# Sums, splits and means around the output projection of a hybrid encoder layer: three reorderings

## Chip, cores and metric

The kernel runs on one core of one Trainium2 chip. The metric is the time of one execution on the device in microseconds; three runs of the kernel before gave a median of 774.31 us (773.64 to 775.06). Lower is better.

## What is computed

One layer for 512 prompt frames and 32 sample frames (544 columns; D_MODEL 1024, D_FF 4096), all in float32:

```
xn = RMSNorm(x);  [u | q | k | v | gate_a | gate_b] = xn @ w_in
A = pooling mixer(u): trailing means of 2/4/8/16 rows less the row, a 128x128 map per group, scaled
B = stick-breaking attention(q, k, v), 8 heads of 64, strictly causal, cached keys for the samples
x += (sigmoid(gate_a) * (A @ w_pool_up) + sigmoid(gate_b) * (B @ w_sb_up)) @ w_out
x += relu(RMSNorm(x) @ w_up)^2 @ w_down
x += sigmoid(RMSNorm(x) @ w_ple_gate) * (p @ w_ple_proj);  y = final RMSNorm(x)
```

## The kernel before

Features lie on the 128 partitions, the 544 columns on the free axis, in two halves of 272. Each float32 operand is split into a high part in fp32r and a low part (the rest), and TensorE does three matmuls per product: high by high, high by low, low by high. Weights come in tiles of 128x1024 (512 KB). SyncE loads a tile into a raw buffer; ScalarE copies its high part (`split` and `hi`, lines 836 to 854); VectorE subtracts it to get the low part (lines 1808 to 1822); TensorE uses it. `ahead(t)` on ScalarE and VectorE makes the parts of tile t+3; there are four tiles of parts (W_RING) and, until the MLP, two raw buffers; from there on six.

The order of work is written out by hand for each engine in one block (SyncE from line 637, GpSimd 707, ScalarE 833, TensorE 1323, VectorE 1799); the engines meet at counting semaphores alone. `full` counts results that TensorE has finished, `taken` those that VectorE has taken out of PSUM, `copied` those that ScalarE has; a result uses one of four PSUM slots, and `place_for` (line 1610) or `take` (line 1330) makes TensorE wait until the slot's former result is out.

The stages in order of time: the input projection with attention, a pair of heads at a time (`pair`: ScalarE 960, TensorE 1467, VectorE 1989); the pool projection (`pool_part`, line 1448) and the attention projection; the output projection, eight tiles w_out, q = 0 to 7; the MLP; the embedding gate; the last norm. The MLP and the gate use a scheme of seven products per 2x2 block (Strassen-Winograd), in groups of seven (`group_of`, line 1661); it needs four sums of weight quarters for each group.

**The last pair of heads.** On VectorE it ends with gate(3, i), stick(1, i), group_lo(2), group_lo(3), stick_later(1, i), a split and stick_lo(1, i) (lines 2063 to 2072). `group_lo(g)` takes the mixer map of group g out of PSUM, after ScalarE's `group_hi(g)` (line 955). `stick` takes the logarithms of the last head; then GpSimd masks them (line 763), ScalarE makes their high part (`stick_hi`), and TensorE sums them (`sums(1, PAIRS - 1)`) after the first two tiles of the pool projection.

**The sums of quarters.** GpSimd makes them in DRAM in 19 slots: `sum_copies(k)` (line 775) issues four copies of group k, once all DMAs of slot k-1 have landed; `sum_additions(k)` (line 784) issues the four additions of the groups k-1, k-2 and k-3. Slots 0 to 7 are issued in the pairs of heads, 8 to 18 in a loop over `paces` (lines 811 to 821), a pair of counts of `full` for each slot: one that its copies wait for, one that its additions wait for. Slot 9 waits for the attention projection, slot 10 for the output projection, 11 and on for every half chunk of the MLP. SyncE loads sums from there into raw buffers (`staged`, line 673), up to nine products before they are used.

**The output projection.** For each tile q, VectorE adds the result to x (`add_residual`, line 2137, "the residual" below). Then eight operands of the MLP are made from two feature tiles each: ScalarE scales x by the norm's weight (lines 1068 and 1074), VectorE forms differences (lines 2156 to 2169), ScalarE makes high parts (1071 to 1081) and a square (869), VectorE the low parts (`low`, line 2147) and the sum of squares. ORDER pairs tiles, so that even q have the operands B11 and NT1, odd q the others. The split of the weight tile q+4 stands ahead of this work on both engines: line 1089 on ScalarE (ahead of its wait for the residual), line 2153 on VectorE (behind the residual). The same helper `operand_lo` serves the last down projection with nth = 1.

In the first up group ScalarE copies the first three results out of PSUM (`copy_quarter`, line 1093), the first of these once all low operands are made (line 1151); the third product of a group adds onto the PSUM slot of the first.

Of the kernel before, what the change touches and what calls it, by code (L numbers as in the profile page):

```python
# [28 lines left out]
KT = D_MODEL // P  # L29
# [268 lines left out]
def hybrid_step_kernel(nc, w_tiles, x_t, p_t, ck_t, cv, state_t, w_grp, vecs,  # L298
# [5 lines left out]
    with ctx:  # L304
# [402 lines left out]
        def _(pool):  # L707
# [100 lines left out]
                                   base=0, pattern=[[0, HEADS], [1, DEC]], channel_multiplier=-1).then_inc(done, 1)  # L808


            paces = [(0, 0), (N_ATT, N_ATT + KT // 2), (N_OUT, N_OUT + KT // 2)]
            for c in range(CHUNKS):
                second = [NTH[("dn", c, s, 0)] for s in (0, 4)] if c < SEVENS else [NTH[("down", c, q)] for q in (0, 4)]
                paces += [(NTH[("up", 2 * c, 0)], NTH[("up", 2 * c + 1, 0)]), tuple(second)]
            for k, (copies, additions) in enumerate(paces, HEADS):
                if copies:
                    pool.wait_ge(full, copies)
# [15 lines left out]
        def _(act):  # L833
# [251 lines left out]
            act.wait_ge(blo_done, KT)  # L1085
            ahead(T_OUT)
            for q in range(KT):
                if q < KT - 1:
                    ahead(T_OUT + q + 1)
                act.wait_ge(taken, N_OUT + q + 1)  # L1090
                operand_hi(0, q, g_mlp)

            def copy_quarter(g, n, s):

# [704 lines left out]
        def _(dve):  # L1799
# [8 lines left out]
            def split(t, i=0, per=0):  # L1808

                s = t % W_RING  # L1810
                dve.wait_ge(whi_done, t + 1 + i * per)
                dve.tensor_tensor(w_lo[:, s, :, :].rearrange("p k c -> p (k c)"), raw[:, t % RAW_RING, :],  # L1812
                                  w_hi[:, s, :, :].rearrange("p k c -> p (k c)"), ALU.subtract).then_inc(wlo_done, 1)
# [80 lines left out]
            def stick(hh, i):  # L1894

                g = 2 * i + hh
                dve.wait_ge(ln_done, g + 1)
                dve.scalar_tensor_tensor(out=work[:, :], in0=z_ps, scalar=0.0, in1=work[:, :],
                                         op0=ALU.max, op1=ALU.add).then_inc(sp_done, 1)
# [89 lines left out]
            def pair(i):  # L1989
                first = isinstance(i, int) and i == 0  # L1990
                last = isinstance(i, int) and i == PAIRS - 1
                q, k, v = (ev[:, n, 0:TOK] for n in range(3))
                if not first:
                    split(AHEAD + 0, i, S1_PER)

                dve.wait_ge(full, 1 + i * S1_PER)
                dve.scalar_tensor_tensor(out=halves(q), in0=pair_result(0, i), scalar=DH ** -0.5, in1=halves(rn[:, :]),
                                         op0=ALU.mult, op1=ALU.mult).then_inc(taken, 1)
                if first:
                    normed(1, k, i, S1_PER, pair_result(1, i)).then_inc(taken, 1)  # L2000
                    normed(2, v, i, S1_PER, pair_result(2, i)).then_inc(taken, 1)
                    dve.wait_ge(taken, 3)
                if first:
                    q_parts(i)
                    k_parts(i)
                    pool_input(i)
                    split(AHEAD + 1)
                    running_q(i)
                    dve.tensor_copy(kst[:, i, :], k[:, SEQ:TOK])
                    dve.tensor_copy(vst[:, i, :], v[:, SEQ:TOK])  # L2010
                    split(AHEAD + 2)
                else:
                    running_q(i)
                    q_parts(i)
                    split(AHEAD + 1, i, S1_PER)
                    dve.wait_ge(kv_out[0], 16 * i)
                    normed(1, k, i, S1_PER, pair_result(1, i)).then_inc(taken, 1)
                    dve.wait_ge(taken, 2 + i * S1_PER)
                    dve.tensor_copy(kst[:, i, :], k[:, SEQ:TOK])
                    k_parts(i)  # L2020
                    split(AHEAD + 2, i, S1_PER)
                    prob_lo(1, i - 1)
                    dve.wait_ge(kv_out[1], 16 * i)
                    normed(2, v, i, S1_PER, pair_result(2, i)).then_inc(taken, 1)
                    dve.wait_ge(taken, 3 + i * S1_PER)
                    dve.tensor_copy(vst[:, i, :], v[:, SEQ:TOK])
                if not first:
                    head_out(1, i - 1)
                    stick(0, i)
                    split(AHEAD + 3, i, S1_PER)  # L2030
                    stick_later(0, i)

                if not first:
                    pool_input(i)
                if first:
                    stick(0, i)
                    split(AHEAD + 3)
                    stick_later(0, i)
                stick_lo(0, i)
                dve.wait_ge(vhi_done, i + 1)  # L2040
                dve.tensor_tensor(v_parts[:, :, V_LO, :], o_heads, v_parts[:, :, V_HI, :], ALU.subtract)\
                   .then_inc(vlo_done, 1)
                split(AHEAD + 4, i, S1_PER)
                gate(0, i)
                split(AHEAD + 5, i, S1_PER)
                if last:

                    dve.wait_ge(mean_done, GROUPS)
                gate(1, i)
                split(AHEAD + 6, i, S1_PER)  # L2050
                if last:
                    mean_lo(0)
                    mean_lo(1)
                prob_lo(0, i)
                gate(2, i)
                if last:
                    group_lo(0)
                head_out(0, i)
                if last:
                    group_lo(1)  # L2060
                    mean_lo(2)
                    mean_lo(3)
                    gate(3, i)
                else:
                    split(AHEAD + 7, i, S1_PER)
                stick(1, i)
                if last:
                    group_lo(2)
                    group_lo(3)
                    stick_later(1, i)  # L2070
                    split(AHEAD + 7, i, S1_PER)
                    stick_lo(1, i)
                    for s in kv_out:
                        dve.wait_ge(s, 16 * PAIRS)
                else:
                    gate(3, i)
                    stick_later(1, i)
                    stick_lo(1, i)
# [62 lines left out]
            def operand_lo(nth, q, t):  # L2141


                m, j = ORDER[q], ORDER[q] % 4
                of = 3 * (KT // 2 * nth + j)

                def low(first, last, at, made):
                    dve.wait_ge(uhi_done, made)
                    dve.tensor_tensor(u_lo[:, first:last + 1, j, :], parts[:, at:at + last - first + 1, :],
                                      u_hi[:, first:last + 1, j, :], ALU.subtract).then_inc(ulo_done, 1)  # L2150

                if q < KT - 1:
                    ahead(t + 1)
                dve.wait_ge(xg_done, KT * nth + q + 1)
                if m < 4:
                    dve.tensor_tensor(parts[:, P_NT1, :], parts[:, P_B11, :], parts[:, P_B12, :], ALU.subtract)\
                       .then_inc(t_done, 1)
                    if q:
                        add_square(q - 1, (nth + 1) * KT)
                    low(NT1, B11, P_NT1, of + 1)  # L2160
                else:
                    dve.scalar_tensor_tensor(out=parts[:, P_NT2, :], in0=parts[:, P_B22, :], scalar=-1.0,
                                             in1=parts[:, P_NT1, :], op0=ALU.mult, op1=ALU.subtract)\
                       .then_inc(t_done, 1)
                    link(dve.tensor_tensor(parts[:, P_T3, :], parts[:, P_B22, :], parts[:, P_B12, :], ALU.subtract))
                    dve.wait_ge(t_done, of + 2)
                    dve.scalar_tensor_tensor(out=parts[:, P_T4, :], in0=parts[:, P_NT2, :], scalar=-1.0,
                                             in1=parts[:, P_B21, :], op0=ALU.mult, op1=ALU.subtract)\
                       .then_inc(t_done, 1)
                    if q < KT - 1:  # L2170
                        add_square(q - 1, (nth + 1) * KT)
                    low(B21, NT2, P_B21, of + 2)
                    low(T3, T4, P_T3, of + 3)
                if q == KT - 1:
                    add_square(q - 1, (nth + 1) * KT)
                    add_square(q, (nth + 1) * KT)

            ahead(T_OUT)
            for q in range(KT):
                add_residual(N_OUT + q, ORDER[q])  # L2180
                operand_lo(0, q, T_OUT + q)

            def add_quarter(g, n, s):

# [369 lines left out]
```

## Time and profile before

| | |
|---|---|
| median of three runs | 774.31 us (773.64 to 775.06) |
| the profiled execution: its own time | 772.34 us |
| its span, first to last instruction | 770.6 us |
| TensorE busy | 754.8 us, 5902 matmuls |
| VectorE busy | 556.9 us |
| ScalarE busy | 422.0 us |
| GpSimd busy | 147.2 us |
| mean granted TensorE clock | 0.996 |

PE is TensorE, DVE VectorE, ACT ScalarE, POOL GpSimd. Times in a timeline are from the start of the span. A name like L2139 is a line of the kernel; `x2` merges neighbouring instructions. In brackets stands how long the engine was idle before the instruction and what released it.

### The profile page before, as it was taken

The numbers are of one execution on the slowest core, as the hardware profiler recorded it, in microseconds if no ns is written. First come the engines' busy times: TensorE is split into PE (matmuls) and PEld (weight loads), VectorE is DVE, ScalarE is ACT, GpSimd is POOL, SyncE is SP. The second block draws the span as 40 slices with busy tenths as digits, with TensorE's granted clock in tenths as the row PEclk, the third lists the DMA queues.
The fourth block names the chain that finished last, engine by engine and source line by source line (L and its number), as shares of the span: only waits on it lengthen the run. The fifth ranks groups of instructions, "written<-read, shape, count | busy, mean of one in ns | idle before, by whom it ended". The sixth has DMA issues, their size and how long they took to land.

```text
span 770.6 us, 14459 instructions
## 1 busy us (share of the span) xinstructions
PE 754.8 (98%) x5902; PEld 746.2 (97%) x5902; DVE 556.9 (72%) x705; ACT 422.0 (55%) x524; POOL 147.2 (19%) x259
## 2 busy tenths in 40 slices
PE   9999999999999999999999999999999999999994
PEld 9999999999999999999999999999999999999993
DVE  6776556566567527588998669965998667677986
ACT  7545535435485442477674347634763356556575
POOL 1051342453471332021110111111101000000001
PEclk9999999999999999999999999999999999999998
DMA  7254848769779899988797989789776957342503
GB/s 242 93 181 140 233 147 224 225 193 262 218 179 265 259 242 275 292 267 262 213 299 270 236 329 251 282 232 354 207 243 201 278 185 217 105 117 66 204 1 116
DMA packets 49516, 165.78 MB, mean 215 GB/s; under 512 B 6320, under 2 KB 8368, under 8 KB 49456
## 3 DMA queue, kind: packets, MB, share of 16 engines
q1 hardware_dynamic: 28512, 94.16, 35.6%
q0 software_dynamic: 18688, 67.18, 35.5%
q10 hardware_dynamic: 2256, 3.60, 1.4%
q8 instruction: 43, 0.70, 0.4%
q14 instruction: 17, 0.14, 0.1%
HBM read 160.39 MB, written 71.63 MB: 301 GB/s over the span
## 4 chain that ended last, share of the span: by engine, by line
PE 90%; DVE 5%; ACT 3%; issue 1%; DMA 1%; SPq 0%; POOL 0%; POOLq 0%; DVEq 0%
PE psum L1646 23%; PE psum L1697 16%; PE psum L1345 14%; PE psum L1351 14%; PE psum L1348 14%; PE psum L1394 1%; PE psum L1422 1%; DMA xt<-x_t 1%; PE psum L1420 1%; PE psum L1382 1%; PE psum L1381 1%; ACT xt L1265 1%; PE psum L1401 1%; PE psum L1406 1%; ACT L879 0%
## 5 line engine op out<-in xcount | busy, mean ns | idle before, releaser
L853 ACT ACTIVATE w_hi<-raw_more 128x1024 fp32r<-128x1024 f32 x83 | 87.7, 1056 | 72.3 <-PE psum L1697 43.3
L1345 PE MATMUL psum<-a_hi,w_hi 128*128 128x272 f32 x576 | 120.6, 291 | 0.6 <-DVE w_lo L1812 0.5
L1820 DVE TENSOR_TENSOR w_lo<-raw_more,w_hi 128x1024 fp32r<-128x1024 f32 x83 | 101.1, 1222 | 26.1 <-ACT w_hi L853 25.7
L1351 PE MATMUL psum<-a_hi,w_lo 128*128 128x272 f32 x576 | 119.3, 289 | 0.0
L1348 PE MATMUL psum<-a_lo,w_hi 128*128 128x272 f32 x576 | 118.9, 288 | 0.0
L1646 PE MATMUL psum<-u_hi,w_hi 128*128 128x272 f32 x560 | 116.4, 289 | 1.0 <-ACT h_of L1097 1.0
L1646 PE MATMUL psum<-u_hi,w_lo 128*128 128x272 f32 x560 | 115.8, 289 | 0.0
L1646 PE MATMUL psum<-u_lo,w_hi 128*128 128x272 f32 x560 | 115.7, 288 | 0.0
L1345 PEld LDWEIGHTS psum<-a_hi,w_hi 128*128 128x128 f32 x576 | 90.3, 189 | 1.1 <-DVE w_lo L1812 0.7
L1348 PEld LDWEIGHTS psum<-a_lo,w_hi 128*128 128x128 f32 x576 | 90.5, 189 | 0.0
L1351 PEld LDWEIGHTS psum<-a_hi,w_lo 128*128 128x128 f32 x576 | 90.0, 189 | 0.0
L1646 PEld LDWEIGHTS psum<-u_hi,w_hi 128*128 128x128 f32 x560 | 87.9, 188 | 1.7 <-issue 1.2
L1646 PEld LDWEIGHTS psum<-u_lo,w_hi 128*128 128x128 f32 x560 | 88.3, 189 | 0.0
L1646 PEld LDWEIGHTS psum<-u_hi,w_lo 128*128 128x128 f32 x560 | 87.4, 188 | 0.0
L1812 DVE TENSOR_TENSOR w_lo<-raw,w_hi 128x1024 fp32r<-128x1024 f32 x41 | 51.2, 1250 | 43.3 <-ACT w_hi L845 43.1
L1820 DVE TENSOR_TENSOR w_lo<-raw,w_hi 128x1024 fp32r<-128x1024 f32 x44 | 53.6, 1222 | 19.2 <-ACT w_hi L853 12.3
L789 POOL DMA_DIRECT2D sums_t<-sums_t x32 | 27.5, 1013 | 207.1 <-PE psum L1646 87.9
L1348 PE MATMUL psum<-b_lo,w_hi 128*128 128x272 f32 x304 | 62.9, 288 | 0.0
L853 ACT ACTIVATE w_hi<-raw 128x1024 fp32r<-128x1024 f32 x39 | 41.2, 1056 | 36.0 <-PE psum L1697 21.6
L1345 PE MATMUL psum<-b_hi,w_hi 128*128 128x272 f32 x288 | 60.0, 290 | 0.0
L782 POOL DMA_DIRECT2D sums_t<-w_tiles x64 | 33.6, 535 | 135.5 <-DMA sums_t<-w_tiles 97.7
L1351 PE MATMUL psum<-b_hi,w_lo 128*128 128x272 f32 x288 | 59.4, 287 | 0.0
(287 smaller groups left out, 1553.0 us busy)
## 6 DMA issues: line engine op xcount, KB each, us to landing
sums_t<-w_tiles POOLq DMA_DIRECT2D x96, 512.0 KB, 8.2
raw<-w_tiles SPq DMA_DIRECT2D x63, 512.0 KB, 4.4
raw_more<-sums_t SPq DMA_DIRECT2D x42, 512.0 KB, 5.8
raw_more<-w_tiles SPq DMA_DIRECT2D x41, 512.0 KB, 4.5
sums_t<-sums_t POOLq DMA_DIRECT2D x32, 512.0 KB, 11.1
raw<-sums_t SPq DMA_DIRECT2D x22, 512.0 KB, 6.0
xt<-x_t SPq DMA_DIRECT2D x8, 272.0 KB, 5.7
y_t<-xt SPq DMA_DIRECT2D x16, 136.0 KB, 1.9
```

What stands on the lines that cost most here:

```text
L782: pool.dma_start(sum_tile(i, what), sum_tile(i, of)).then_inc(sums_in, 16)
L789: pool.dma_start(sum_tile(i, what), sum_tile(i, of), accum_op=ALU.add).then_inc(sums_in, 16)
L853: act.activation(w_hi[:, t % W_RING, :, :].rearrange("p k c -> p (k c)"), src, ACT.Copy)\
L1265: act.activation(x, x, ACT.Copy, scale=g_fin[:, m:m + 1]).then_inc(xg_last, 1)
L1345: pe.matmul(base[:, h, :], w_hi[:, s, wk, :], at(hi, k, h * HALF, (h + 1) * HALF), start=(opens and q == 0), stop=False, skip_group_check= ...
L1348: pe.matmul(base[:, h, :], w_hi[:, s, wk, :], at(lo, k, h * HALF, (h + 1) * HALF), start=False, stop=False, skip_group_check=True)
L1351: mm = pe.matmul(base[:, h, :], w_lo[:, s, wk, :], at(hi, k, h * HALF, (h + 1) * HALF), start=False, stop=(closes and q == len(ks) - 1), s ...
L1381: pe.matmul(z, b_lo[:, keys], b_hi[:, both], start=(b != 3), stop=False, skip_group_check=True)
L1646: mm = pe.matmul(out[:, two, :], w_part[:, t % W_RING, 2 * k + two, :], u_part[:, op, k, :], start=(OPENS[s] and k == 0 and w_part is w_hi ...
L1697: mm = pe.matmul(out[:, two, :], w_part[:, t % W_RING, 2 * k + two, :], h_part[:, i * HALF:(i + 1) * HALF], start=(OPENS[s] and k == 0 and ...
L1812: dve.tensor_tensor(w_lo[:, s, :, :].rearrange("p k c -> p (k c)"), raw[:, t % RAW_RING, :], w_hi[:, s, :, :].rearrange("p k c -> p (k c)" ...
L1820: dve.tensor_tensor(w_lo[:, t % W_RING, :, :].rearrange("p k c -> p (k c)"), src, w_hi[:, t % W_RING, :, :].rearrange("p k c -> p (k c)"), ...
```

## The change

The constants of the slots' waits are written anew: counted in products from the start of the MLP, with `at(c, j)` the j-th product of chunk c, and no slot waits for the output projection any more. On ScalarE and VectorE the split of tile q+4 in the output projection moves behind the operand work of tile q. In the last pair of heads group_lo(2) moves ahead of stick(1).

```diff
@@ -808,10 +808,18 @@
-            paces = [(0, 0), (N_ATT, N_ATT + KT // 2), (N_OUT, N_OUT + KT // 2)]
-            for c in range(CHUNKS):
-                second = [NTH[("dn", c, s, 0)] for s in (0, 4)] if c < SEVENS else [NTH[("down", c, q)] for q in (0, 4)]
-                paces += [(NTH[("up", 2 * c, 0)], NTH[("up", 2 * c + 1, 0)]), tuple(second)]
+            def at(c, j):
+
+                if j < 2 * T_UP:
+                    return NTH[("up", 2 * c + j // T_UP, j % T_UP)]
+                j -= 2 * T_UP
+                return NTH[("dn", c, j // 2, j % 2)]
+
+            paces = [(0, 0), (N_ATT, N_ATT + KT // 2)]
+            paces += [(at(0, 0), at(0, 6)), (at(0, 12), at(0, 18)), (at(0, 24), at(1, 1)), (at(1, 6), at(1, 12)),
+                      (at(1, 18), at(1, 23)), (at(2, 2), at(2, 8)), (at(2, 14), at(2, 20)),
+                      (at(3, 2), at(3, 8)), (NTH[("down", 3, 0)], NTH[("down", 3, 4)])]
             for k, (copies, additions) in enumerate(paces, HEADS):
                 if copies:
                     pool.wait_ge(full, copies)
@@ -1085,10 +1093,11 @@
             for q in range(KT):
+                act.wait_ge(taken, N_OUT + q + 1)
+                operand_hi(0, q, g_mlp)
+
                 if q < KT - 1:
                     ahead(T_OUT + q + 1)
-                act.wait_ge(taken, N_OUT + q + 1)
-                operand_hi(0, q, g_mlp)
@@ -2063,9 +2072,11 @@
+                if last:
+
+                    group_lo(2)
                 stick(1, i)
                 if last:
-                    group_lo(2)
                     group_lo(3)
                     stick_later(1, i)
                     split(AHEAD + 7, i, S1_PER)
@@ -2149,7 +2160,7 @@
-                if q < KT - 1:
+                if nth and q < KT - 1:
                     ahead(t + 1)
                 dve.wait_ge(xg_done, KT * nth + q + 1)
@@ -2179,6 +2190,8 @@
             for q in range(KT):
                 add_residual(N_OUT + q, ORDER[q])
                 operand_lo(0, q, T_OUT + q)
+                if q < KT - 1:
+                    ahead(T_OUT + q + 1)
```

## Rows read from the trace of the kernel before

**Rows 1.** The page: busy time of TensorE; its granted clock in 40 slices.

```profile
PE 754.8 (98%) x5902; PEld 746.2 (97%) x5902; DVE 556.9 (72%) x705; ACT 422.0 (55%) x524; POOL 147.2 (19%) x259
...
PEclk9999999999999999999999999999999999999998
```

**Rows 2.** Waits of TensorE: us in total, times, longest.

```profile
PE psum L1781 <- ACT h_two L1310: 1.9, 1, 1.9
...
PE psum L1646 <- ACT h_of L1097: 1.0, 1, 1.0
```

**Rows 3.** Timeline of TensorE, 234 to 256 us: start, us, engine, line, operation.

```profile
245.09 0.49 PE L1345 MATMUL psum<-mean_hi,w_hi 128*128 128x272 f32 x2 [1.11 <-issue]
...
251.19 0.40 PE L1394 MATMUL psum<-b_hi,negtri 128*128 128x512 f32 x1
```

**Rows 4.** Timeline of VectorE, 236 to 256 us.

```profile
242.82 1.48 DVE L1898 SCALAR_TENSOR_TENSOR work<-psum,work 128x1280 f32<-128x1280 f32 x1
244.21 1.47 DVE L1985 SCALAR_TENSOR_TENSOR b_lo<-psum,vec,b_hi 128x544 fp32r<-128x544 f32 x2
245.60 0.29 DVE L1905 TENSOR_TENSOR later<-work 128x128 f32<-128x128 f32 x1
...
248.74 0.55 DVE L1915 TENSOR_TENSOR later_lo<-later,later_hi 128x384 fp32r<-128x384 f32 x1
```

**Rows 5.** Timeline of ScalarE, 236 to 256 us.

```profile
242.93 0.72 ACT L957 ACTIVATE b_hi<-psum,vec 128x544 fp32r<-128x544 f32 x1 [0.74 <-PE psum L1328]
```

**Rows 6.** Timeline of GpSimd, 236 to 256 us.

```profile
244.37 1.02 POOL L767 TENSOR_SCALAR_AFFINE_SELECT work<-work 128x128 f32<-128x128 f32 x4 [10.46 <-DVE work L1898]
```

**Rows 7.** Timeline of VectorE in the output projection, 290 to 390 us.

```profile
319.83 0.72 DVE L2139 TENSOR_TENSOR xt<-psum,xt 128x544 f32<-128x544 f32 x1
...
342.43 0.72 DVE L2139 TENSOR_TENSOR xt<-psum,xt 128x544 f32<-128x544 f32 x1
343.07 1.22 DVE L1820 TENSOR_TENSOR w_lo<-raw_more,w_hi 128x1024 fp32r<-128x1024 f32 x1
344.20 0.43 DVE L2156 TENSOR_TENSOR h_of<-h_of 128x272 f32<-128x272 f32 x1
...
346.86 1.23 DVE L1820 TENSOR_TENSOR w_lo<-raw_more,w_hi 128x1024 fp32r<-128x1024 f32 x1
...
355.45 0.72 DVE L2139 TENSOR_TENSOR xt<-psum,xt 128x544 f32<-128x544 f32 x1 [0.43 <-PE psum L1351]
357.00 0.44 DVE L2162 SCALAR_TENSOR_TENSOR h_of<-h_of 128x272 f32<-128x272 f32 x1 [0.82 <-ACT h_of L1074]
```

**Rows 8.** Timeline of ScalarE in the output projection, 290 to 390 us.

```profile
323.11 1.06 ACT L845 ACTIVATE w_hi<-raw 128x1024 fp32r<-128x1024 f32 x1 [4.46 <-DMA raw<-w_tiles]
...
343.19 0.75 ACT L1068 ACTIVATE h_of<-xt,vec 128x544 f32<-128x544 f32 x1 [0.67 <-DVE xt L2139]
...
345.78 1.04 ACT L853 ACTIVATE w_hi<-raw_more 128x1024 fp32r<-128x1024 f32 x1
...
356.22 0.75 ACT L1074 ACTIVATE h_of<-xt,vec 128x544 f32<-128x544 f32 x1 [1.40 <-DVE xt L2139]
...
359.42 1.04 ACT L853 ACTIVATE w_hi<-raw_more 128x1024 fp32r<-128x1024 f32 x1
360.37 0.60 ACT L1097 ACTIVATE h_of<-psum 128x544 f32<-128x544 f32 x1
```

**Rows 9.** Chain that ended last, in order of time: start, us, what.

```profile
355.42 9.05 PE psum L1646 x72
...
383.65 0.63 ACT h_of L1097
384.42 15.41 PE psum L1646 x120
```

**Rows 10.** Timeline of GpSimd, 225 to 420 us: first copy of slots 9 and 10.

```profile
303.32 2.07 POOL L782 DMA_DIRECT2D sums_t<-w_tiles  x4 [17.57 <-DMA sums_t<-w_tiles]
...
330.50 1.57 POOL L782 DMA_DIRECT2D sums_t<-w_tiles  x3 [21.71 <-DMA sums_t<-w_tiles]
```

## The prediction

> **What bounds the kernel now.** The page comes first, its parts 1 and 2: TensorE is busy 98% of the span, and the granted clock stands at 9 in 39 of the 40 slices and at 8 in the last [rows 1]. So only holes in TensorE's stream can give time, and only new holes can take it. The list of TensorE's waits shows how few there are; the longest are 1.9 us at the very end and 1.0 us on the ScalarE copy of line 1097 [rows 2]. The timeline adds one that no wait explains, 1.11 us before 245.09 us, and the chain of waits tells which of them matter.
>
> The hole at 245.09 us is where the first tile of the pool projection begins [rows 3]. That tile (pool_part(0)) goes into the PSUM slot that the third group of means left, so it waits for group_lo(2). On VectorE this runs behind stick(1): the stick at 242.82 us, then group_lo(2) and (3) from 244.21 us, 1.47 us for the two [rows 4]. TensorE starts 0.14 us after the first of them has ended (244.21 + 0.74 = 244.95).
>
> The other is at 384.42 us: the third product of the second up group waits for the copy that began at 383.65 us [rows 9]. The chain of waits leads from there through VectorE and ScalarE alone back to the end of the third product of the first up group, 355.42 + 9.05 = 364.47 us [rows 9], so what delays that product delays everything behind it. In the output projection itself (307 to 355 us) TensorE never waits; only ScalarE and VectorE run late there: the residual of the first tile is added at 319.83 us, that of the last at 355.45 us, just when TensorE has made it [rows 7].
>
> **Third group ahead of the sticks.** VectorE comes to this place at 242.82 us, but group_lo(2) needs ScalarE's group_hi(2), which ends at 242.93 + 0.72 = 243.65 us [rows 5]. So group_lo(2) can run from 243.68 to 244.42 us, and TensorE starts at 244.56 instead of 245.09: 0.53 us won. What is queued behind it pays: stick(1) starts at 244.33 instead of 242.82 us and ends at 245.81; group_lo(3) ends at 246.5 us, before TensorE asks for it (18 matmuls in, 246.8 us); GpSimd's masks take 1.02 us, from 0.07 us after the stick [rows 6], so they end at 246.90. From there VectorE's block from stick_later to the end of stick_lo takes 248.74 + 0.55 - 245.60 = 3.69 us [rows 4] and ends at 250.64 us. TensorE wants it after two tiles, before at 251.19 us [rows 3], now at 250.66 us. No lead is left, and with the 0.14 us from signal to matmul some 0.1 us is given back. I take a gain of 0.4 us. Bounds: 0.53 us at best; nothing, or a loss of some tenths, if the masks or the ScalarE copy between them take longer than in these rows.
>
> **The slot of sums.** Slot 10 (four copies and four additions issued by GpSimd, 512 KB each) leaves 330.50 us and waits for the first up product, its additions for the seventh. But the stage is not empty of sums by that: slot 9 is issued from 303.32 us, and the 21.71 us that slot 10 waited ended only when slot 9 had landed [rows 10]. The weight load that holds ScalarE until 323.11 us [rows 8] falls under slot 9, which stays. After 330 us no split waits for a load, so slot 10's going is worth nothing here. In the MLP the slots then come every 10 to 12 products instead of 14, but for the last two. GpSimd has nothing else queued there, and the last addition to each group is still issued six products or more before the first load that needs it. Six raw buffers cover slower loads: the list of waits names no DMA ahead of line 853 in the whole MLP. I cost it at nothing. If that cover went, a load might hold ScalarE for the 4.46 us of [rows 8]; but three weight tiles, 9 us of products, are split ahead of TensorE, so both ends stay near 0.
>
> **Operands ahead of the splits.** This is the term that decides. Before, ScalarE makes the high part of weight tile q+4 before it waits for residual q, and VectorE makes the low part while ScalarE scales x. After, both do it last. So VectorE's subtraction waits for ScalarE's operands, square and high part, and residual q+1 waits for that subtraction: one serial chain. Its length comes from steps between starts in the rows.
>
> An even q (B11, NT1): residual to scaled x 0.76 (342.43 to 343.19); scaled x to VectorE's difference 0.78 (356.22 to 357.00); from that over u_hi and the square to the high part 1.58 (344.20 to 345.78); high part to low part 1.08 (345.78 to 346.86); low part to the next instruction 1.13 (343.07 to 344.20). Sum 5.33 us [rows 7, 8].
>
> An odd q (the other operands): residual to high part 3.97 (355.45 to 359.42, where nothing stood between), then 1.08 and 1.13. Sum 6.18 us [rows 7, 8].
>
> Four even and three odd steps lie between the first and the last residual: 4 x 5.33 + 3 x 6.18 = 39.9 us. The first stays at 319.83 us (the split before it is not moved). So the last comes at 359.7 us instead of 355.45: 4.2 us late. The old order took 13.0 us for the last three steps (342.43 to 355.45), the new one 16.8 (two even, one odd), and TensorE makes three tiles in 18, so the lag from the beginning is hardly worked off.
>
> Who waits: the second up product takes the PSUM slot of that last residual, so it starts some 2 us late. The third adds onto the slot of the first, so it needs the copy of line 1097, which follows the last residual by 4.92 us (355.45 to 360.37) [rows 7, 8]: 364.6 us; and TensorE follows a copy's start by 0.77 us (383.65 to 384.42) [rows 9]: 365.4 us. Before, it started at 355.42 + 2/3 of 9.05 = 361.45 us [rows 9]. That is 3.9 us lost, in two stalls of about 2 us. The chain from there to 384.42 us is the old one, moved by as much, so the 1.0 us there stays; and behind it TensorE is the bound, so nothing is caught up. Bounds: each of the seven steps 0.1 us shorter gives 3.2 us, the first load 0.5 us later still 4.4 us.
>
> Two stalls raise the question of the clock. The wait of 1.9 us near the end [rows 2] left no slice but the last below 9 [rows 1], so I add nothing. The Trainium skill, "TensorE: Matmul & The Clock Gate", section "What's actually happening", has an idle TensorE throttled to 1.2 GHz until it has been active again. By that rule the sum could be some us longer; the rows do not show it for a wait of this size.
>
> **Sum.** -0.4 + 0 + 3.9 = +3.5 us (I take the gain at 245 us to move all that follows, the first residual too). The profiled execution took 772.34 us for its span of 770.6, so 775.8 on its scale. It lies 2.0 us under the median of the runs, 774.31. On the median's scale: 777.8 us.
>
> **The rivals.** (A) Not slower: the chain is not serial, because the low part on VectorE still finds its high part ready. It decides at 5.13 us a step ((355.76 - 319.83) / 7): below that the third product starts on time. Then 773.9 us remains, or 772.9 if earlier operands also take away the 1.0 us at 384 us. For it: the old order needed 4.3 us a step at the end. Against it: both queues are in order, and the new order puts the high part behind the square and the residual behind the low part. 13%.
>
> (B) The lag is half hidden, a step at 5.4 us: the last residual at 357.6, the third product at 363.3, 1.9 us lost, less 0.4: 775.8 us. It needs operations shorter than in the rows. 10%.
>
> (C) The stalls throttle TensorE: a product of 3.02 us (a third of 9.05) then takes twice that, one or two of them: 781 to 784 us. Against it stands the wait of 1.9 us [rows 2]. For it speaks only the page named above. 5%.
>
> (D) The change does not do what it says: slot 9's traffic still lies under the output projection [rows 10]. This is part of the forecast, not a case beside it.
>
> **How the numbers follow.** Forecast 72%: 777.8 us; its bounds and the spread of the runs (773.64 to 775.06) make that 776.4 to 779.2. The range of 8 in 10 takes in the forecast and most of B: 774.8 to 779.5. A measurement of this kernel can tell about 0.2% (1.5 us) from no change. Faster by that (under 772.8): the lower half of A, 7%. Within: its upper half, and nine tenths of B, 15%. Slower (over 775.9): the forecast, C and B's rest, 78%.
>
> **What would show it.** In the new profile: pool_part(0) starts some 0.5 us nearer to the matmul before it; stick(1) stands behind group_lo(2); the starts of line 2139 lie 5.3 and 6.2 us apart in turn, the last near 359 us; TensorE has two new waits in the first up group, before its second product (on line 2139) and its third (on line 1097), about 2 us each; no wait on a DMA in the MLP; clock 9 but for the last slice. I am wrong if the last residual comes within half a us of TensorE's tile, or if TensorE's stream shows a new hole past 400 us.

## The result, and the profile after

The changed kernel takes 777.38 us (median of 7 runs, 776.92 to 778.23) where the kernel before took 775.06 us beside it (7 runs, 773.64 to 776.61): a ratio of 1.0033, 95% interval 1.0021 to 1.0045. It is slower, by 2.3 us between the medians and 2.6 us by the ratio. The profiled execution of after took 777.8 us for its span of 776.1.

The page of after, parts 1 and 2, answers [rows 1]:

```profile
PE 755.9 (97%) x5902; PEld 746.3 (96%) x5902; DVE 557.9 (72%) x705; ACT 422.3 (54%) x524; POOL 146.3 (19%) x259
...
PEclk9999999999999999999999999999999999999997
```

TensorE works 1.1 us longer in a span that is 5.5 us longer: the time went into holes, stretches in which TensorE stands idle. The list of TensorE's waits (us in total, times, longest), against [rows 2]:

```profile
PE psum L1655 <- DVE w_lo L1829: 2.8, 2, 1.7
PE psum L1790 <- ACT h_two L1319: 1.9, 1, 1.9
PE psum L1655 <- issue: 1.5, 1, 1.5
...
PE psum L1655 <- ACT h_of L1106: 1.0, 1, 1.0
```

The 1.9 us at the end and the 1.0 us on the copy (L1097 before, L1106 now) are the old ones. The first and the third line are new. TensorE's timeline shows where they are, and the hole of [rows 3]:

```profile
244.90 0.49 PE L1354 MATMUL psum<-mean_hi,w_hi 128*128 128x272 f32 x2 [0.58 <-issue]
...
251.08 0.50 PE L1403 MATMUL psum<-b_hi,negtri 128*128 128x512 f32 x1
...
356.55 0.49 PE L1655 MATMUL psum<-u_hi,w_hi 128*128 128x272 f32 x2 [1.16 <-DVE w_lo L1829]
...
361.89 0.49 PE L1655 MATMUL psum<-u_hi,w_hi 128*128 128x272 f32 x2 [1.65 <-DVE w_lo L1829]
...
366.68 0.49 PE L1655 MATMUL psum<-u_hi,w_hi 128*128 128x272 f32 x2 [1.54 <-issue]
...
389.88 0.49 PE L1655 MATMUL psum<-u_hi,w_hi 128*128 128x272 f32 x2 [1.02 <-ACT h_of L1106]
```

At 244.90 us the hole is 0.58 us, where it was 1.11. At 356.55, 361.89 and 366.68 us the first, second and third up product wait. The third starts 5.2 us later than the 361.45 us worked out for before (the timeline of before has it at 361.29 us), although the first residual stands where it stood (319.81 and 319.83 us).

The chain that ended last shows the stall between the second and the third product, in a stretch that was one piece in [rows 9]:

```profile
361.89 3.24 PE psum L1655 x24
365.13 1.54 issue
366.68 3.26 PE psum L1655 x24
...
389.88 15.41 PE psum L1655 x120
```

VectorE in the output projection, against [rows 7] (the residual is L2150 now, the low part of a weight tile L1829):

```profile
319.81 0.72 DVE L2150 TENSOR_TENSOR xt<-psum,xt 128x544 f32<-128x544 f32 x1
...
326.45 0.72 DVE L2150 TENSOR_TENSOR xt<-psum,xt 128x544 f32<-128x544 f32 x1
...
349.56 0.72 DVE L2150 TENSOR_TENSOR xt<-psum,xt 128x544 f32<-128x544 f32 x1
...
355.74 0.72 DVE L2150 TENSOR_TENSOR xt<-psum,xt 128x544 f32<-128x544 f32 x1
357.27 0.44 DVE L2167 TENSOR_TENSOR h_of<-h_of 128x272 f32<-128x272 f32 x1 [0.82 <-ACT h_of L1076]
...
359.93 1.23 DVE L1829 TENSOR_TENSOR w_lo<-raw_more,w_hi 128x1024 fp32r<-128x1024 f32 x1 [0.77 <-ACT w_hi L861]
361.07 0.72 DVE L2150 TENSOR_TENSOR xt<-psum,xt 128x544 f32<-128x544 f32 x1
```

ScalarE beside it, against [rows 8]:

```profile
324.21 1.06 ACT L853 ACTIVATE w_hi<-raw 128x1024 fp32r<-128x1024 f32 x1 [1.18 <-DMA raw<-w_tiles]
...
356.49 0.75 ACT L1076 ACTIVATE h_of<-xt,vec 128x544 f32<-128x544 f32 x1 [1.93 <-DVE xt L2150]
...
358.31 0.64 ACT L877 ACTIVATE ev<-xt 128x544 f32<-128x544 f32 x1
358.86 1.04 ACT L861 ACTIVATE w_hi<-raw_more 128x1024 fp32r<-128x1024 f32 x1
...
365.97 0.60 ACT L1106 ACTIVATE h_of<-psum 128x544 f32<-128x544 f32 x1
```

The serial chain is there to be read: residual 355.74, scaled x 356.49, difference 357.27, square 358.31, high part of the weights 358.86, their low part 359.93, next residual 361.07. Steps of 6.18 us (odd q) and 5.33 us (even q, one of them 5.43) follow each other; only the first is longer, 6.64 us, for ScalarE waits 1.18 us for its load. In the list of waits the second product is put down to the low part of L1829, but that ended 0.73 us earlier; the last residual ended at 361.07 + 0.72 = 361.79 us, 0.10 us ahead of the product. The first product waits in the same way for the seventh residual (355.74 + 0.72 = 356.46, start 356.55).

GpSimd's slots, against [rows 10]:

```profile
301.87 2.07 POOL L782 DMA_DIRECT2D sums_t<-w_tiles  x4 [16.52 <-PE psum L1360]
...
355.70 1.57 POOL L782 DMA_DIRECT2D sums_t<-w_tiles  x3 [48.37 <-PE psum L1360]
```

Slot 9 is still under the output projection; slot 10 has left it.

### The profile page after: what moved, and what is told of

Its sections match the earlier page's. It is cut to its first block, busy times and chain, and to the rows that moved or that the text cites. A ratio compares the mean times of both kernels' runs of the same rounds, so it can differ in the third digit from the quotient of the medians.

```text
span 776.1 us, 14459 instructions
## 1 busy us (share of the span) xinstructions
PE 755.9 (97%) x5902; PEld 746.3 (96%) x5902; DVE 557.9 (72%) x705; ACT 422.3 (54%) x524; POOL 146.3 (19%) x259
## 4 chain that ended last, share of the span: by engine, by line
PE 75%; DVE 8%; issue 7%; ACT 6%; DMA 2%; POOL 1%; POOLq 0%; SPq 0%; DVEq 0%
PE psum L1655 23%; PE psum L1706 16%; PE psum L1354 10%; PE psum L1360 10%; PE psum L1357 9%; DMA raw<-w_tiles 2%; DVE w_lo L1829 2%; PE psum L1403 1%; ACT w_hi L853 1%; ACT w_hi L861 1%; PE psum L1431 1%; PE psum L1429 1%; ACT gates L960 1%; PE psum L1391 1%; DVE gates L2142 1%
## 5 line engine op out<-in xcount | busy, mean ns | idle before, releaser
L1829 DVE TENSOR_TENSOR w_lo<-raw_more,w_hi 128x1024 fp32r<-128x1024 f32 x83 | 101.1, 1222 | 27.4 <-ACT w_hi L861 27.1
L1829 DVE TENSOR_TENSOR w_lo<-raw,w_hi 128x1024 fp32r<-128x1024 f32 x44 | 53.6, 1221 | 17.3 <-ACT w_hi L861 12.3
```

Source lines behind the costliest of these rows:

```text
L1829: dve.tensor_tensor(w_lo[:, t % W_RING, :, :].rearrange("p k c -> p (k c)"), src, w_hi[:, t % W_RING, :, :].rearrange("p k c -> p (k c)"), ...
```

## The experiments

Each kernel had 20 to 34 runs of before beside it; the parts alone were measured on one chip, the next four kernels on a second, the last two on a third. So a ratio goes by the before beside it, and a difference of medians is surest within such a group. "The old slots" are those of before.

**The parts alone.** Order alone:

```diff
             for q in range(KT):
-                if q < KT - 1:
-                    ahead(T_OUT + q + 1)
                 act.wait_ge(taken, N_OUT + q + 1)
                 operand_hi(0, q, g_mlp)
+                if q < KT - 1:
+                    ahead(T_OUT + q + 1)
...
-                if q < KT - 1:
+                if nth and q < KT - 1:
                     ahead(t + 1)
...
                 operand_lo(0, q, T_OUT + q)
+                if q < KT - 1:
+                    ahead(T_OUT + q + 1)
```

> Only the split of tile q+4 is moved behind the operands of tile q, on ScalarE and VectorE; the slots of sums and the means stay as before. Theory 1 (the loss is the serial chain): slower than before by as much as the whole change or 0.4 us more, 2.5 to 4.5 us in the medians; residual starts 5.3 and 6.2 us apart in turn, the last at 359 to 361 us, TensorE waits of about 2 us ahead of the second and the third up product. Theory 2 (the loss comes from the slots of sums, which crowd the loads of the MLP): within 0.5 us of before. Theory 3 (the loss comes from the sticks, which come 1.5 us later): within 0.5 us of before.

Measured: 778.96 us (777.1 to 780.39), ratio 1.005, interval 1.0031 to 1.0068: 3.9 us slower by the ratio, 3.6 us between the medians. TensorE's new waits are those of after (1.11, 1.65 and 1.53 us).

Slots alone: the `paces` of the change, with the rest as before.

> Only the waits of the slots of sums are changed, as in the change. Theory 1: within 0.5 us of before, no wait of ScalarE on a DMA in the MLP, the last residual within 0.5 us of TensorE's tile. Theory 2: slower by 2 to 3 us, with TensorE or ScalarE waiting for loads after 400 us. Theory 3: within 0.5 us of before.

Measured: 772.75 us (772.36 to 773.83), ratio 0.9966, interval 0.9952 to 0.998: 2.6 us **faster**, where the prediction has nothing. And yet the profile of this kernel looks much like the first profile of before; of the first up group it has one hole of 0.15 us:

```profile
361.47 0.48 PE L1653 MATMUL psum<-u_hi,w_hi 128*128 128x272 f32 x2 [0.15 <-issue]
```

Means alone: group_lo(2) ahead of stick(1), with the rest as before.

> Only group_lo(2) stands ahead of stick(1), as in the change. Theory 1: faster by 0.3 to 0.5 us, the first tile of the pool projection 0.5 us nearer to the matmul before it, and some 0.1 us of wait ahead of the last sums of the sticks. Theory 2: the same. Theory 3: slower by 1 us or more, with a wait of TensorE at the sums of the sticks.

Measured: 774.26 us (771.56 to 776.26), ratio 0.9983, interval 0.9967 to 0.9999. The hole falls to 0.58 us. The size drowns in the spread of the old slots, so it is measured again below.

**Where do 2.6 us come from, if the profile of before has no hole for them?** Its own time, 772.34 us, lies 2.7 us under the median of before in the comparison with after. So the kernel before was profiled once more, unchanged:

> The kernel before, unchanged, for a second profile of it, since its first profiled execution (772.34 us) lies 2.7 us under the median of its seven timed runs (775.06). If the spread comes from the loads of the output projection: 774 to 776 us, with a first weight load of the stage that lands later than 323.1 us, residuals later than in the first profile and a longer wait of TensorE in the first up groups. If it comes from elsewhere (the start, or the clock): the stage from 307 to 400 us as in the first profile, and the difference ahead of it or behind it.

Measured: 776.89 us, span 775.1: 4.55 us more than the first profiled execution of the same kernel. TensorE in the first up group of this second profile of before:

```profile
357.40 0.49 PE L1646 MATMUL psum<-u_hi,w_hi 128*128 128x272 f32 x2 [1.58 <-issue]
...
360.30 0.52 PE L1646 MATMUL psum<-u_hi,w_hi 128*128 128x272 f32 x2 [0.38 <-DVE u_lo L2149]
...
365.76 0.48 PE L1646 MATMUL psum<-u_hi,w_hi 128*128 128x272 f32 x2 [1.45 <-issue]
```

These 3.4 us are not in the first profile at all. (Another 0.4 us of the 4.55 lie ahead of the pool projection: its first tile starts at 245.50 us here, at 245.09 us there.) ScalarE's timeline of the second profile says why, and GpSimd's and SyncE's behind it:

```profile
326.08 1.06 ACT L845 ACTIVATE w_hi<-raw 128x1024 fp32r<-128x1024 f32 x1 [7.03 <-DMA raw<-w_tiles]
...
342.03 1.06 ACT L845 ACTIVATE w_hi<-raw 128x1024 fp32r<-128x1024 f32 x1 [3.36 <-DMA raw<-w_tiles]
```

```profile
329.38 1.57 POOL L782 DMA_DIRECT2D sums_t<-w_tiles  x3 [21.10 <-DMA sums_t<-w_tiles]
```

```profile
332.23 0.33 SPq L690 DMA_DIRECT2D raw<-w_tiles  x1
```

The load at 332.23 us is that of the last tile w_out. Here it is issued 2.85 us after slot 10's first copy. The view of that one issue gives its landing, in the second profile of before:

```profile
DMA to landing us min/median/max: 9.8/9.8/9.8
```

In the first profile SyncE issued the same load at 330.50 us, the same time as slot 10's first copy [rows 10]. The same view of it there:

```profile
DMA to landing us min/median/max: 4.0/4.0/4.0
```

So slot 10 can hold up the output projection: where that load comes behind it, it takes 9.8 us instead of 4.0, ScalarE waits 3.36 us, and the residuals end late. But the first load of the stage is late in the second profile too: ScalarE waits 7.03 us for it, against 4.46 us. Two other profiles tell the two apart. In the slots alone the first load is as late (6.71 us), but the last load takes 3.5 us, and the hole is the 0.15 us above. In the means alone the first load is nearly that of the first profile (4.96 us), but the last one, issued at 329.77 us behind slot 10 at 328.27 us, takes 9.8 us again. ScalarE waits for it, and then TensorE for the third product:

```profile
339.57 1.06 ACT L845 ACTIVATE w_hi<-raw 128x1024 fp32r<-128x1024 f32 x1 [3.36 <-DMA raw<-w_tiles]
```

```profile
363.29 0.48 PE L1646 MATMUL psum<-u_hi,w_hi 128*128 128x272 f32 x2 [1.44 <-issue]
```

With 0.24 and 0.38 us ahead of it, its holes come to 2.1 us. So the late last load alone costs TensorE some 2 us, and 3.4 us where the first load is late as well. The first profile of before was an execution without it.

**Slots and means together, without the order.** All of the change but its order.

> The change without its new order of splits: the new waits of the slots, and group_lo(2) ahead of stick(1). If the parts add up: 2.6 us (slots alone) and 0.4 to 1.1 us (means alone) faster than before, a ratio of 0.995 to 0.996, and some 5 to 6 us faster than the whole change. If the means only gained by moving the loads against slot 10: no faster than the slots alone, 0.9966.

Measured: 772.65 us (771.77 to 773.57), ratio 0.997, interval 0.9957 to 0.9983. Against the whole change (1.0033) the order costs 1.0033 / 0.997, that is 0.63% or 4.9 us (4.7 us between the medians, and as much between the spans of the two profiles, 776.1 and 771.4 us), more than the 3.9 us predicted. Beside the slots alone the means bring nothing here: this execution waits longer for the first load (7.42 us against 6.71 on ScalarE), and the third product has a hole of 0.79 us. Slot 9 is the next suspect.

**No slot at all in the output projection.** From the kernel with the slots alone:

```diff
-            paces = [(0, 0), (N_ATT, N_ATT + KT // 2)]
-            paces += [(at(0, 0), at(0, 6)), (at(0, 12), at(0, 18)), (at(0, 24), at(1, 1)), (at(1, 6), at(1, 12)),
-                      (at(1, 18), at(1, 23)), (at(2, 2), at(2, 8)), (at(2, 14), at(2, 20)),
+            paces = [(0, 0), (at(0, 0), at(0, 5)), (at(0, 10), at(0, 15)), (at(0, 20), at(0, 25)), (at(1, 2), at(1, 7)),
+                     (at(1, 12), at(1, 17)), (at(1, 22), at(1, 27)), (at(2, 4), at(2, 9)), (at(2, 14), at(2, 20)),
                      (at(3, 2), at(3, 8)), (NTH[("down", 3, 0)], NTH[("down", 3, 4)])]
```

> The old order of splits and means; no slot of sums between the attention projection and the MLP (slot 9 waits for the first up product too, slots 10 to 15 follow every 10 products). If slot 9 is what makes the first weight load of the output projection late: that load lands by 318 us, no wait of ScalarE on a DMA in the stage, the second residual at 324 to 325 us instead of 327 to 330. If the order of slots costs nothing once the last residual meets TensorE on time: the time of the slots alone, ratio 0.996 to 0.997, since slot 9 delays only residuals that the old order works off.

Measured: 772.72 us (771.62 to 773.79), ratio 0.9977, interval 0.9967 to 0.9988. VectorE now waits for TensorE at the residuals, not the other way round:

```profile
349.82 0.73 DVE L2145 TENSOR_TENSOR xt<-psum,xt 128x544 f32<-128x544 f32 x1 [0.25 <-PE psum L1357]
355.82 0.72 DVE L2145 TENSOR_TENSOR xt<-psum,xt 128x544 f32<-128x544 f32 x1 [1.82 <-PE psum L1357]
```

But its median is that of the slots alone (772.75 us; the intervals of the two ratios overlap): with slot 10 gone, slot 9's late load is made good before the stage ends. This kernel has no load wait in the stage, so the order can be measured on it by itself.

**The order without any slot.** The diff of the order alone, on the kernel just shown.

> As e6, with the splits behind the operands on both engines, so that the stage has no DMA but its own loads. If the serial chain is the loss: steps of 5.33 and 6.18 us in turn from 319.8 us, the last residual at 359.7 us, and 3.9 us slower than e6 (ratio near 1.002). If the new order only lost because slot 9 made its first load late (rival): the last residual within 0.5 us of TensorE's tile, and the time of e6.

Measured: 777.19 us (776.38 to 777.58), ratio 1.0034, interval 1.0022 to 1.0046: 4.5 us above the kernel it is made from. First and last two residuals, and then TensorE:

```profile
320.51 0.72 DVE L2145 TENSOR_TENSOR xt<-psum,xt 128x544 f32<-128x544 f32 x1
...
355.14 0.72 DVE L2145 TENSOR_TENSOR xt<-psum,xt 128x544 f32<-128x544 f32 x1
360.48 0.71 DVE L2145 TENSOR_TENSOR xt<-psum,xt 128x544 f32<-128x544 f32 x1
```

```profile
361.30 0.49 PE L1652 MATMUL psum<-u_hi,w_hi 128*128 128x272 f32 x2 [1.66 <-DVE w_lo L1826]
...
366.08 0.48 PE L1652 MATMUL psum<-u_hi,w_hi 128*128 128x272 f32 x2 [1.54 <-issue]
```

39.97 us lie between the first and the last residual; the prediction's seven steps make 39.9. The chain costs this with no transfer in the way.

**Which engine's order costs it?** The split behind the operands on VectorE alone; on ScalarE the high part stays ahead.

```diff
-                if q < KT - 1:
+                if nth and q < KT - 1:
                     ahead(t + 1)
...
                 operand_lo(0, q, T_OUT + q)
+                if q < KT - 1:
+                    ahead(T_OUT + q + 1)
```

> As e6, with the split behind the operands on VectorE alone; ScalarE makes the high part ahead of its wait for the residual, as before. If the chain is serial because ScalarE's high part lies between VectorE's operands and its subtraction: the steps shrink by 0.85 us (even q) and 0.1 us (odd q) to 4.5 and 6.1 us, the last residual at 356 us, less than 1 us slower than e6. If it is the residual's place behind VectorE's subtraction that matters: steps and time as in e7.

Measured: 772.74 us (772.02 to 773.13), ratio 0.9977, interval 0.9965 to 0.9989: no cost at all against 772.72. The last residuals of this kernel:

```profile
350.80 0.72 DVE L2145 TENSOR_TENSOR xt<-psum,xt 128x544 f32<-128x544 f32 x1
355.29 0.72 DVE L2145 TENSOR_TENSOR xt<-psum,xt 128x544 f32<-128x544 f32 x1
```

Steps of 4.5 and 5.7 to 6.1 us in turn: since ScalarE's high part lies ready, the low part follows the operands directly. So the chain closes only with ScalarE's part of the move. That part by itself has no run: with VectorE's subtraction in its old place it would stand still, each engine waiting for what the other has queued behind.

**A version that beats both.** Old order, no slot in the output projection, means ahead of the sticks.

> Old order of splits and operands, no slot of sums in the output projection at all, and the third group of means ahead of the sticks. My theory, that the three parts are independent and additive: 0.4 us under the kernel with slot 9 late alone (772.7), so about 772.3 us, a ratio of 0.997 to the kernel before; the hole ahead of the first tile of the pool projection falls from 1.1 to about 0.6 us; no hole of TensorE in the first up group. Rival, that the gain at 245 us is taken back by the last sticks, which then come late: a new wait of TensorE on the sums of the last sticks, and no gain.

Measured: 772.03 us (771.3 to 772.9, 9 runs), before beside it 774.85; ratio 0.9965, interval 0.9953 to 0.9977. It is 0.7 us under the kernel without the means, near what the hole gives (1.11 to 0.58 us), and no wait on the last sticks comes up. It is the fastest median of the study and beats the kernel before and the changed one; against the kernels at 772.7 us the difference is no more than their spread.

The 1.0 us at 384 us was tried on top of it:

```diff
                         operand_low(g - 1, "NT1")
-                    ahead(t_up(g, s))
+                        if g == 1:
+                            ahead(t_up(0, T_UP - 1))
+                    if (g, s) != (0, T_UP - 1):
+                        ahead(t_up(g, s))
```

> The same, and VectorE's split for the last product of the first up group moves behind the first low operand of the second. My theory: VectorE's 1.13 us of split no longer stands in the chain from the first up group's results to the first low operand of the second, so TensorE's wait of 1.0 us on the third product's ScalarE copy falls to about 0.3 us; 0.7 us less than the kernel beside it, about 771.6 us. Rival, that the chain runs over ScalarE's operands alone: the wait stays at 1.0 us and the time with it. Second rival: the later split makes TensorE wait for its low weights, a new wait on line 1829 or near it.

Measured: 773.35 us (772.26 to 773.9), ratio 0.9985, interval 0.9974 to 0.9997: worse than the kernel beside it. VectorE's split, moved, and TensorE:

```profile
382.68 1.22 DVE L1826 TENSOR_TENSOR w_lo<-raw_more,w_hi 128x1024 fp32r<-128x1024 f32 x1
```

```profile
383.95 0.52 PE L1652 MATMUL psum<-u_hi,w_hi 128*128 128x272 f32 x2 [1.00 <-DVE w_lo L1826]
...
387.86 0.48 PE L1652 MATMUL psum<-u_hi,w_hi 128*128 128x272 f32 x2 [0.64 <-ACT h_of L1103]
```

The second rival held. The copy does come 0.45 us earlier (382.79 us, 383.24 beside it), but the split that made room for it makes the low weights of just that product, so TensorE waits the same 1.0 us for those, and 0.64 us more for the next copy. These 0.6 us are half of what the medians differ by; the other half stays open.

## Why the prediction came out right, and where it was wrong

It said 777.8 us and slower; measured were 777.38 us and slower. The order's mechanism is shown, but the closeness of the total rests on terms that were off in opposite directions.

**Operands ahead of the splits: right in kind, sized too small.** Predicted were 3.9 us; on the same slots and means it cost 4.7 us between the medians (4.9 by the ratios), and 4.5 us with no slot in the way. The steps hold to 0.1 us: 5.33 and 6.18 us in the rows of after, 39.97 us for all seven in the kernel without slots. There the working holds nearly whole: from the first residual to the third product it takes 45.57 us (366.08 - 320.51), just as predicted (365.4 - 319.83), and 41.42 us in the same kernel with the old order (361.66 - 320.24). These 4.15 us are 0.2 more than the prediction's difference, because the third product of before starts at 361.29 us and not at 361.45; the remaining 0.3 of the 4.5 us stay open. In after the first step was too small on top of it: "The first stays at 319.83 us" was right, but the load late under slot 9 came in only as 0.5 us of the bound. By [rows 8] it is there at 323.11 us, just when ScalarE now comes to it (324.21 - 1.18 = 323.03); in after it came 1.18 us later. The old order works such a delay off, a serial chain keeps it, and it is in the first step (6.64 us). The last residual thus came at 361.07 us instead of 359.7, and the third product at 366.68 instead of 365.4. One wait was not named: the first up product, on the seventh residual (1.16 us); without slots the first product has no such wait, so it belongs to the late load. (In the order alone it waits 1.11 us, and there the late load is slot 10's: 10.5 us to landing, 1.14 us of wait on ScalarE at 342.78 us.) The second and third product wait as predicted, for 1.65 and 1.54 us. The copy's wait at 384 us stayed (1.02 us, now at 389.88 us), as predicted.

**The slot of sums: wrong.** The failed step is "After 330 us no split waits for a load, so slot 10's going is worth nothing here." It was true of the execution read, and not of the kernel: slots alone gave 2.6 us (ratio 0.9966), and a second execution of before shows the wait that the slot causes. The warning stood in the numbers: the execution lay 2.0 us under the median, and the prediction added these 2.0 us back as if they were a constant that any kernel would carry. By the profiles they were, in the main, what slot 10 costs. Adding them and leaving out the gain are one error: slot 10's wait is missing from the execution read, it is in the median, and it goes with the slot. It put the forecast 2.0 us too high. Against it stand two that put it too low: slots and means without the order take 772.65 us, 0.7 us more than 772.34 - 0.4, and the order costs 0.8 us more than 3.9. That these nearly cancel, and leave 0.4 us, is luck. The difference itself was forecast at 3.5 us, and 2.3 to 2.6 us were measured. The denser slots in the MLP cost nothing, as predicted, and gain nothing: in after ScalarE waits for no load past 365 us, and from the product that waits at 384.42 us in before to the end of the span it takes 386.2 us there (770.6 - 384.42), 386.1 in the slots alone (770.8 - 384.67) and 386.2 in after (776.1 - 389.88).

**Third group ahead of the sticks: right at the hole.** It falls by 0.53 us, as worked out; the sticks followed in the order and at the distances given (VectorE and then GpSimd in after, against [rows 4, 6]):

```profile
244.01 0.78 DVE L1994 SCALAR_TENSOR_TENSOR b_lo<-psum,vec,b_hi 128x544 fp32r<-128x544 f32 x1 [0.78 <-ACT b_hi L965]
244.71 1.48 DVE L1907 SCALAR_TENSOR_TENSOR work<-psum,work 128x1280 f32<-128x1280 f32 x1
...
250.47 0.55 DVE L1924 TENSOR_TENSOR later_lo<-later,later_hi 128x384 fp32r<-128x384 f32 x1
```

```profile
246.26 1.03 POOL L767 TENSOR_SCALAR_AFFINE_SELECT work<-work 128x128 f32<-128x128 f32 x4 [12.03 <-DVE work L1907]
```

The last stick's sums start at 251.08 us in after, 6.18 us after the pool projection's first tile, where they started 6.10 us after it [rows 3]: 0.1 us given back, as predicted (the working had a slip of 0.05 us: 246.90 + 3.69 is 250.59). What it brings in the medians is not settled: 0.7 us without slots, nothing beside the slots alone.

**The rivals.** (A) fell: a step takes 5.33 to 6.18 us, not under 5.13, because ScalarE's high part moved too; where it stayed ahead, the steps measure 5.10 us on average ((355.29 - 319.57) / 7, the first residual of that kernel at 319.57 us), just under the 5.13 us at which A decides, and nothing is lost. (B) fell by the same rows. (C) fell: three stalls of 1.2 to 1.7 us lie between 355 and 367 us, and the granted clock of after is 1.00 from 356 to 360, from 360 to 365.2 and from 365.2 to 370 us, the level of 2.4 GHz; the second product takes 3.24 us and the third 3.26, against 3.02 in the prediction, not twice that. The rule of the Trainium skill, "TensorE: Matmul & The Clock Gate", section "What's actually happening", by which an idle TensorE is throttled, took nothing here for stalls of this size. (D) holds: slot 9 stayed, and the order's chain waited 1.2 us for it. Between the medians this hardly shows: with slot 9 and the means 777.38 us, without both 777.19. With the old order its going was worth nothing that the medians show (772.72 against 772.75 us).

The sum as measured, each as its ratio times 775 us: slots and means -2.3, order on top of them +4.9, together +2.6 us. The parts alone give -2.6, -1.3 and +3.9, together 0.0: the parts do not add up. The likely reason is that with slot 10 in place the old order is late too, so that the order costs less. How far the means' -1.3 is theirs cannot be told; its interval reaches from -2.6 to -0.1 us, and the hole says 0.5.

## What to carry to other kernels

When two in-order engines hand work to and fro, the work that waits for nothing (a high part of weights that have landed) belongs ahead of the wait, or it joins the chain with its whole length, and every late load with it. When a profiled execution lies below the median by as much as the terms that are being priced, take a second one before pricing a transfer at nothing: the wait may come in other executions and be missing in the one that is read. A term that cancels another by chance is found only by trying the parts alone.

## What was not expected of the hardware

The same 512 KB load took 4.0 us when it was issued with the first copy of a slot of sums, 9.8 us (means alone) and 10.5 us (order alone) 1.5 us behind it, 9.8 us 2.85 us behind it (second profile of before), and 3.5 to 3.6 us with no slot there (slots alone, slots and means, after). Why so small a lead of the slot matters so much stays open. The late load holds up an execution of before by 2 to 3.4 us of TensorE's time. The runs fit that: with slot 10 they spread over 5.2 us (before, 772.23 to 777.39 over 34 runs), 4.7 us (means alone) and 3.3 us (order alone), the kernels without it over 1.1 to 2.2 us. That the wait makes the whole spread is argued from the profiles, not shown run by run.
